# Moving three blocks of the stick-breaking projections, and giving the memory stage's projections banks of their own

## What is computed

```python
h = _rmsnorm(x, g_pre); proj = h @ w_in
# stick-breaking, 8 heads of 64, strictly causal
z = q @ k.T * scale; log_1mb = where(strict, log_sigmoid(-z), 0)
between = cumsum(log_1mb, reverse) - log_1mb
y_sb = where(strict, exp(log_sigmoid(z) + between), 0) @ v * silu(g)
# differential attention, 4 heads: partial rotary on q and k, two softmaxes, p0 - lam * p1
# memory, 4 heads of 64
mkv = _rmsnorm(mem, g_mem) @ w_mem_kv
y_m = softmax(mq @ mk.T * scale) @ mv * silu(m_g)
x + _rmsnorm(concat(y_sb, y_df, y_m) @ w_out, g_post)
```

## Time and profile before

| what | us |
|---|---|
| median of 3 runs | 2133.34 |
| the profiled execution, its own time | 2134.68 |
| span in the profile | 2132.9 |
| PE busy | 1897.1 (89%) |
| DVE busy | 1346.2 (63%) |
| ACT busy | 1085.5 (51%) |
| POOL busy | 549.9 (26%) |

### The profile page before, as it was taken

One profiled execution on the slowest core, in us unless ns is written; L12 is line 12 of the kernel. 1 busy time (PEld: TensorE's weight loads), 2 busy tenths in 40 slices (PEclk: granted clock), 3 DMA queues, 4 the chain that ended last, 5 costly groups with the idle time before them and its releaser, 6 DMA issues.

```text
span 2132.9 us, 34211 instructions
## 1 busy us (share of the span) xinstructions
PE 1897.1 (89%) x11552; PEld 1600.2 (75%) x11552; DVE 1346.2 (63%) x2807; ACT 1085.5 (51%) x2406; POOL 549.9 (26%) x436
## 2 busy tenths in 40 slices
PE   6999997899999999999998689888488888888998
PEld 6999997777777777777787577766366666667886
DVE  7606885676767676766766613334578888874544
ACT  6422111665666566666656523333377878872221
POOL 0000000343434444444444300011134444440000
PEclk9999998898989898999999779999689999999999
DMA  6322131001010000101000112133801313014542
GB/s 219 96 69 64 65 117 49 6 6 25 5 25 12 18 18 13 24 6 25 5 25 6 45 50 78 53 116 107 190 3 37 74 28 82 8 64 174 183 153 79
DMA packets 121866, 129.28 MB, mean 61 GB/s; under 512 B 81936, under 2 KB 94992, under 8 KB 120464
## 3 DMA queue, kind: packets, MB, share of 16 engines
q1 hardware_dynamic: 121744, 127.86, 20.6%
HBM read 85.89 MB, written 41.94 MB: 60 GB/s over the span
## 4 chain that ended last, share of the span: by engine, by line
PE 67%; DVE 15%; ACT 7%; issue 7%; DMA 2%; POOL 1%; SPq 0%; DVEq 0%; ACTq 0%; POOLq 0%
PE ps L647 6%; PE ps L601 6%; PE ps L603 5%; PE ps L602 5%; PE ps L588 4%; PE ps L589 4%; PE ps L590 4%; PE ps L633 4%; DVE small L1480 3%; PE ps L826 3%; PE ps L875 3%; PE ps L877 3%; PE ps L876 3%; PE ps L621 3%; PE ps L784 2%
## 5 line engine op out<-in xcount | busy, mean ns | idle before, releaser
L1623 POOL TENSOR_TENSOR ring_r<-ring,sp_hi 128x512 fp32r<-128x512 f32 (+1 forms) x320 | 358.5, 1120 | 838.0 <-DVE sp_hi L1343 838.0
L647 PEld LDWEIGHTS ps<-v,ring 128*128 128x128 f32 x2176 | 303.8, 202 | 37.2 <-issue 13.3
L647 PE MATMUL ps<-v,ring 128*128 128x65 f32 x2176 | 299.9, 280 | 5.0 <-ACT ring L1000 3.3
L988 ACT ACTIVATE ring<-ps 128x512 f32<-128x512 f32 (+1 forms) x320 | 170.5, 533 | 256.2 <-PE ps L622 194.9
L1642 POOL TENSOR_TENSOR p<-p 128x1024 f32<-128x1024 f32 (+4 forms) x96 | 170.5, 1788 | 246.5 <-ACT p L1135 246.5
L601 PE MATMUL ps<-ht_hi,w_hl 128*128 128x512 f32 x448 | 201.1, 449 | 30.1 <-DVE ring L1437 9.7
L588 PE MATMUL ps<-w_hl,ht_hi 128*128 128x256 f32 x768 | 212.9, 277 | 0.7 <-DVE w_hl L1221 0.6
L589 PE MATMUL ps<-w_hl,ht_hi 128*128 128x256 f32 x768 | 212.6, 277 | 0.0
L590 PE MATMUL ps<-w_hl,ht_lo 128*128 128x256 f32 x768 | 212.6, 277 | 0.0
L1340 DVE SCALAR_TENSOR_TENSOR ring<-ring,ps 128x512 f32<-128x512 f32 (+1 forms) x320 | 192.0, 600 | 30.0 <-ACT ring L993 29.2
L1126 ACT ACTIVATE p<-ps,small 128x1024 f32<-128x1024 f32 (+4 forms) x192 | 164.4, 862 | 69.2 <-DVE small L1484 63.2
(11 more groups left out here) (183 smaller groups left out, 3992.4 us busy)
## 6 DMA issues: line engine op xcount, KB each, us to landing
w_raw<-in_w_narrow SPq DMA_DIRECT2D x18, 512.0 KB, 4.1
xb<-in_x SPq DMA_DIRECT2D x16, 512.0 KB, 3.9
gate_scr<-ring SPq DMA_DIRECT2D x64, 128.0 KB, 1.8
w_raw<-rot_scr SPq DMA_DIRECT2D x32, 256.0 KB, 3.6
qk_scr<-w_hl SPq DMA_DIRECT2D x32, 256.0 KB, 3.3
gb<-gate_scr SPq DMA_DIRECT2D x16, 512.0 KB, 3.6
yb<-y_scr SPq DMA_DIRECT2D x16, 512.0 KB, 4.5
xr<-in_x SPq DMA_DIRECT2D x16, 512.0 KB, 4.2
```

Of the source, the lines that this page charges most:

```text
L647: mm = pe.matmul(ps[:, 4 + i % 2, j * (HD + 1):(j + 1) * (HD + 1)], ring[:, 4 + i % 2, j * P:(j + 1) * P], v1[:, kb, :], start=True, stop= ...
L1623: nc.gpsimd.tensor_tensor(ring_r[:, i % 4, j0 * P:], ring[:, i % 4, j0 * P:], sp_hi[:, i % 4, j0 * P:].bitcast(F32), ALU.subtract).then_in ...
```

## The change

Stick-breaking: block 2 of the next head moves to steps 39 to 42 of this one (for the first head it is projected in steps 0 to 3), the blocks 0 and 1 of the next head move from 28 and 36 to 25 and 32, the weight split from 20 to 18. The second DVE subtraction of block 2 is done in step 44, with the first, as the loop ends there.

Memory stage: items alternate between banks 7 and 5 and wait for the item two before; the exchange has bank 6; the transposes have only bank 4; the values go into the back half of bank 0 or 2, for which scores of item i wait for the multiplication of item i-3. Items are packed from slot -1 to 25 in another order. Weight splits come one slot earlier and ahead of the last item's move. The rotary tables have two buffers. The loads of the first differential head are issued at slot 28, ahead of the last six stores to `y_scr`. POOL, not DVE, zeroes the padding.

```diff
-SB_PROJECT = ((0, 2, 5), (0, 3, 14), (1, 0, 28), (1, 1, 36))
-SB_SPLIT = 20
+SB_PROJECT = ((0, 3, 14), (1, 0, 25), (1, 1, 32), (1, 2, 39))
+SB_SPLIT = 18
...
-X_SLOT = (-1, -1, 1, 2, 4, 5, 7, 8, 11, 12, 13, 16, 18, 19, 20, 21, 23, 24, 25, 26, 28, 29, 30, 31)
+X_SLOT = (-1, -1, 0, 1, 3, 4, 5, 6, 7, 8, 9, 10, 12, 13, 14, 15, 17, 18, 19, 20, 22, 23, 24, 25)
+X_BANK = (7, 5)
+X_PAIRED = 6
...
+                if slot == X_SLOT[-1] + 3:
+                    for u in range(2):
+                        sp.wait_ge(qk_out[u], 32 * NT // 2)
+                    sp.wait_ge(x_pj, len(X_ITEMS))
+                    load_qk(0)
+                    load_df_v(0)
...
             for i in range(SB_LEAD):
+                if i == 0:
+                    pe.wait_ge(sp_act, 6)
+                    pe.wait_ge(sp_dve, 4)
+                if i < 4:
+                    project(C_SB, 2, 7, sp_ps, i)
...
             def x_project(e):
-                kind, k, n = X_ITEMS[e]
-                if e:
-                    before = sum(x < e for x in X_D)
-                    if e - 1 in X_D:
-                        pe.wait_ge(df_t2, before)
+
+                if e >= 2:
+                    differential = sum(x <= e - 2 for x in X_D)
+                    if e - 2 in X_D:
+                        pe.wait_ge(df_x, differential)
                     else:
-                        pe.wait_ge(m_qlo, e - before)
-                project(C_X + e // NT, n, 7, x_pj)
+                        pe.wait_ge(m_qlo, e - 1 - differential)
+                project(C_X + e // NT, X_ITEMS[e][2], X_BANK[e % 2], x_pj)
...
                     pe.wait_ge(m_p, max(0, i - 1))
+                    pe.wait_ge(m_y, max(0, i - 2))
...
+                    if i == at + 5 == SB_LEAD + N_ST - 1 and more:
+                        sb_stack_lo(h, ahead * NT + n, 1)
...
+            for x in df_qk[0]:
+                nc.gpsimd.memset(x[3 * DQ:P, :, :].bitcast(F32), 0.0).then_inc(df_pad[0], 1)
```

More of the change, by code:

```diff
@@ L84 @@
 X_M = [e for e, item in enumerate(X_ITEMS) if item[0] == "m"]
-X_SPLIT = {X_SLOT[NT * k + NT - 1] + 1: k + 1 for k in range(N_X - 1)}
+X_SPLIT = {X_SLOT[NT * k + NT - 1]: k + 1 for k in range(N_X - 1)}
 N_MT = (M_H // 2) * SB
@@ L286, in build @@
         m_yout = [sem("m_yout0"), sem("m_yout1")]
-        df_cs, df_x, df_px, df_t1, df_t2, df_x2, df_hi, df_lo, df_scale = (
-            sem("df_" + n) for n in ("cs", "x", "px", "t1", "t2", "x2", "hi", "lo", "scale"))
+        df_x, df_px, df_t1, df_t2, df_x2, df_hi, df_lo, df_scale = (
+            sem("df_" + n) for n in ("x", "px", "t1", "t2", "x2", "hi", "lo", "scale"))
+        df_cs = [sem("df_cs0"), sem("df_cs1")]
         qk_out = [sem("qk_out0"), sem("qk_out1")]
@@ L413, in load_cos_sin @@
             def load_cos_sin(f):
-                if f:
-                    sp.wait_ge(df_t1, f)
-                    sp.wait_ge(df_t2, f)
+                if f >= 2:
+                    sp.wait_ge(df_t1, f - 1)
+                    sp.wait_ge(df_t2, f - 1)
                 n = X_ITEMS[X_D[f]][2]
-                for q, dst in enumerate((cos_c, sin_c)):
-                    sp.dma_start(dst, rot_scr[q, :, n * TQ:(n + 1) * TQ]).then_inc(df_cs, 16)
+                for q in range(2):
+                    sp.dma_start(cos_sin[f % 2][:, q, :], rot_scr[q, :, n * TQ:(n + 1) * TQ]).then_inc(df_cs[f % 2], 16)
             def store_qk(f):
@@ L441, in load_df_v @@
                 sp.dma_start(dst, v_rows[h + SB_H]).then_inc(df_v[h % 2], 16)
-            load_cos_sin(0)
+            for f in range(2):
+                load_cos_sin(f)
             for slot in range(N_MT + 4):
@@ L757, in _ @@
                         for b in range(2):
-                            mm = pe.matmul(ps[:, 6, a * HD:(a + 1) * HD],
+                            mm = pe.matmul(m_values(k)[:, a * HD:(a + 1) * HD],
                                            ring[:, 2 + k % 2, (2 * a + b) * P:(2 * a + b + 1) * P],
@@ L774, in df_scores @@
                 U = s * UNITS + j
+                if s == 0 and j == 0:
+                    pe.wait_ge(m_y, N_MT)
+                    pe.wait_ge(df_x2, len(X_D))
                 if s in (0, 8) and j == 0:
@@ L1031, in _ @@
                 sb_slot(0, i, True)
+            for k in range(3):
+                sb_stack_hi(0, 2, k)
             with act.Fori(0, SB_H - 1) as h:
@@ L1076, in x_move @@
                     act.wait_ge(df_x2, f)
-                nc.scalar.activation(ring[:, X_SRC, :], ps[:, 7, :], ACT.Copy, scale=qk_scale[:]).then_inc(df_x, 1)
+                nc.scalar.activation(ring[:, X_SRC, :], ps[:, X_BANK[e % 2], :], ACT.Copy, scale=qk_scale[:]).then_inc(df_x, 1)
             def x_hi(f):
@@ L1099, in _ @@
                     act.wait_ge(m_o, max(0, k - 1))
-                    nc.scalar.activation(ring[:, 2 + k % 2, :], ps[:, 4 + k % 2, :], ACT.Copy).then_inc(m_pt, 1)
+                    nc.scalar.activation(ring[:, 2 + k % 2, :], ps[:, 4, :], ACT.Copy).then_inc(m_pt, 1)
                 for e in X_AT[i - 1] if i else []:
@@ L1108, in _ @@
                         split_hi(C_X + X_SPLIT[i], NARROW, dc, (x_pj, NT * X_SPLIT[i]))
+                for e in X_AT[i]:
+                    x_move(e)
             def df_exp(s, j):
@@ L1170, in _ @@
             act.wait_ge(m_y, N_MT)
+            for u in range(2):
+                act.wait_ge(qk_out[u], 32 * len(X_D) // 2)
             for s in range(N_SL + 6):
@@ L1390, in _ @@
                 sb_slot(0, i, True)
+            for k in range(2):
+                sb_stack_lo(0, 2, k)
             with dve.Fori(0, SB_H - 1) as h:
@@ L1462, in _ @@
                         x_rotate(X_D.index(e))
+                if i in X_SPLIT:
+                    for dc in range(DC):
+                        split_lo(C_X + X_SPLIT[i], NARROW, dc)
                 for e in X_AT[i]:
@@ L1467, in _ @@
                         x_lo(e)
-                if i in X_SPLIT:
-                    for dc in range(DC):
-                        split_lo(C_X + X_SPLIT[i], NARROW, dc)
             def df_min(s, j):
```

46 lines of the change are left out of this document (22 added, 24 removed).

## The result

The changed kernel takes 2196.03 us (median of 4 runs, 2181.7 to 2216.61) against 2135.56 us of the kernel before (4 runs). The ratio is 1.0256, with a 95% interval of 1.0197 to 1.0315; it leaves out the run of 2216.61, which counts as slow. The forecast was 2152 and its range ended at 2175. The direction was right and most waits came where they were expected; the size was not.

The account below looks back on a forecast made before the run. PE, busy for 89% of the span, was taken as the bound. Stick-breaking +42.7 us and memory stage -24.0 gave +18.7 on 2134.68, 2153.4, or 2152 as a median; 8-in-10 range 2100 to 2175.

Parts of the forecast that it names:

- What goes: Stick-breaking stage: waits of 2.46, 0.62 and 0.72 us and 3.2 of low clock vanish, 7.0 us a head.
- rival 1: The clock holds through the waits of steps 32 and 39: 2111 us, chance 0.20; half of it, 2132, 0.08.
- the 3.2: Work in us lost in one low-clock stretch, as read behind step 12 of a middle head; booked as saved there.
- The waits in steps 32 and 39: New PE waits for bank 7, 3.05 and 3.0 us, each with 2.9 of low clock: +11.85 us a head.
- The seam: Block 2's copies and subtractions ahead of the next head's steps 4 and 5: +2.7 wait, -1.1 clock, net +1.6.
- rival 4: Short gaps, now closer, cost clock too: one more low stretch a head, +20 us, 2172; chance 0.12.
- The first head: First stick-breaking head: no low clock to save, so +3.2 us beyond a loop head's +6.45.
- The memory stage: Stage -20.9 us, wait for differential loads -15.1, last slots held up +11.0, first differential matmul +1.0: -24.0 in all.
- The hold-up by the loads on SP's queue: Last memory slots: `y_scr` stores wait behind 13 loads, +11.0 us, bounds 0 and +13.
- rival 3: Memory stage: the store to `y_scr` passes the loads, -11 us, so 2141; chance 0.10.
- Rivals 1 and 2: Rival 1, and one where PE waits only 0.62 us in steps 32 and 39: 2078 us, chance 0.08.

Follow-up runs that it names:

- block3_early: The changed kernel with block 3 projected in steps 6 to 9 in place of 14 to 17: 2124.11 us, ratio 0.9934.
- block3_early_both: The changed kernel with block 3 in steps 6 to 9, three copies in step at+4 and two subtractions in step at+5: 2062.83 us, ratio 0.9654.
- early_both: The changed kernel with a block's three ACT copies in step at+4 and both DVE subtractions in step at+5: 2161.91 us, ratio 1.0141.
- block3_at10: The changed kernel with block 3 projected in steps 10 to 13 in place of 14 to 17: 2170.19 us, ratio 1.0155.
- experiments 5 and 7: The changed kernel with the weight split at step 20, not 18 (2197.06 us); with block 3 in steps 6 to 9 (2124.11) or 10 to 13 (2170.19).

## Why the prediction was wrong, step by step

**What goes** was right in its waits: those of 2.46, 0.62 and 0.72 are not in the trace of after. Two readings of the low clock behind the 2.46 were not. The prediction says that in the first head the clock held. It fell there too, 1.3 us after the matmul that was read, and stayed low for 6.8 us:

```profile
400.00:402.00 2.00, 1.19 (x7) 1.10 (x8) 1.87 (x6) 0.42 (x1) 0.72 (x1) 1.00 0.00 0
402.00:404.00 2.00, 2.00 (x10) 1.81 (x10) 0.83 (x3) 1.08 (x3) 0.46 (x1) 0.52 0.03 8
404.00:406.00 2.00, 2.00 (x10) 2.00 (x9) 1.34 (x4) 1.39 (x3) 0.63 (x1) 0.50 0.00 0
```

So it was eight heads of eight, the first head had low clock to save, and the row at 400.81 was none for rival 1. And the 3.2 came from a head with a short stretch: behind step 12 the clock is low for 10.2 us in five of the eight heads and for 6.8 in three, so there was more to win than the sum has.

**The waits in steps 32 and 39** were right: 2.86 and 2.65 for 3.05 and 3.0, read off as PE's lead over L1396. Their low clock, 4.5 + 7.4 us a head, costs half, 6.0, for 5.8. What the term as a whole is worth depends on the rest. With the seam covered, taking it away gives 61 us (`block3_early` to `block3_early_both`), with the seam bare 34 (after to `early_both`): the low clock of steps 0 to 17 then grew from 14.8 to 22.8.

**The seam** is the step that failed, in its cause and its size; with it failed what the sum had at nothing, the clock at step 22 (below). I priced the chain of block 2's copies and subtractions at +2.7 of waiting and let the low clock shrink by 1.1. The waiting came out near that, 4.5 us a head in steps 0 to 10 for 2.0 before, but of the 3.3 in step 6 only the 0.9 of the last head is the chain, and the other 2.4 is DVE's loop turn. That was in the trace of before, unpriced: 2.88 us idle ahead of L1354, covered by the very project that the change moves away. I costed the removal from steps 5 to 8 as a pure gain and never asked what it covered. And the clock, low for 6.8 us there before, now stays low for 20 to 24 in three of the six middle heads. So the 3.2 that I booked as saved at step 12 was given back: steps 0 to 17 have 14.8 us of low clock for 15.9, where 4.3 us of work (3.2 + 1.1) were to be won. That the turn and its missing cover do this, and not the chain, is shown by `block3_early` against `block3_at10`, 46 us, and by `early_both`.

**Step 22** was rival 4, taken at 0.12: one more low stretch a head, priced at 2.9. It came in all eight heads, with 9.7 us at low clock in a middle one, up to 4.8 of work. The split's place and block 3's at 14 both act on it (experiments 5 and 7). Why a wait of 1.00 us lowers the clock here, when 0.98 and 0.81 within three did not before, no run settles. The rule of the Trainium skill (page "TensorE: Matmul & The Clock Gate", section "A second HAM failure mode: psum-queue depth-cycling"), that frequent short idles make the clock swing, fits these heads. It gives no size or number of idles, and so does not tell them from those of `block3_early_both`, where a wait of 1.2 us in step 15 passes without a fall in all eight.

Together these terms more than fill the gap: half of the low clock of after, 36.4 us, less half of that of before, 15.9, is +10.2 a head, an upper bound, since PE waits in part of it; forecast +1.5 of clock, measured +8.0.

**The first head** was 21.6 us longer, for 9.7: it is entered 7.5 later, behind a wait for L1396 of 3.45 and the first part of block 2, and has the low stretches of step 22 and of its first steps as well.

**The memory stage** was right: -24.0 forecast, -21.8 to the first differential matmul and -2.6 behind it. The hold-up by the loads on SP's queue, +11.0 with 0 as its other end, was measured at 10.99 on DVE and reached PE as a wait of 9.9, so rival 3 falls.

Rivals 1 and 2 fall as well: the waits came in full, and so did their low clock. The range was too narrow at its top, since rival 4 was priced alone and not together with a seam out of cover.

## What to carry to other kernels

- Before a piece of work is moved, look at what the other engines do while it runs. Here it lay over a gap that no row names: an engine's turn of a loop, 2.1 to 2.9 us "issue" in these two kernels ahead of the first instruction of the body, as often as the loop jumps back. Keep independent work of the bounding engine there.
- Where a buffer's release bounds the next piece, move the last readers ahead in their engines' lists: that was worth 34 us with the seam bare and 61 with it covered.
- Whether the clock fell behind a wait is read from windows of the next few microseconds, not from the first matmul: in the first head it fell 1.3 us later.
- In a kernel whose clock falls behind its waits, sum the waits and the clock apart, and test edits in pairs: two that gave 34 and 72 us alone gave 133 together.

## What was not expected of the hardware

- The loop turn: DVE stands for 2.1 to 2.6 us in the changed kernel, 2.8 to 2.9 before, 1.7 to 3.5 in the other runs where nothing else ends the gap, each time with an 8 KB transfer of instructions about 2 us ahead of its end.
- The clock stays at 1.2 GHz long after the wait that it fell in, with PE recorded as busy throughout:

```profile
514.00:520.00 6.00, 6.00 (x22) 4.70 (x21) 4.93 (x12) 3.16 (x6) 3.85 (x3) 0.50 0.11 22
520.00:526.00 6.00, 6.00 (x27) 5.62 (x26) 2.45 (x7) 2.45 (x6) 2.26 (x2) 0.50 0.00 0
526.00:532.00 6.00, 6.00 (x23) 5.59 (x24) 2.45 (x8) 2.68 (x6) 1.18 (x2) 0.50 0.00 0
```

- Equal heads of one run differ by up to 12 us (109.7 and 121.7 in the changed kernel), with waits that differ by 1 us, by the clock. Runs of one kernel spread by 2 us (`block3_early_both`) to 35 us (the changed one).
